# Taking the next pair's first gate step ahead of the down step in a streamed mixture-of-experts stage

## The reference

```python
D_EXPERT = D_MODEL // 8            # 256
N_EXPERTS = N_GROUPS * EXPERTS_PER_GROUP   # 32, two of them per token
...
h = h + hierarchical_moe(hn, w_router_group[i], w_router_expert[i],
                         w_expert_gate[i], w_expert_up[i], w_expert_down[i])
```

## Time and profile before

| | |
|---|---|
| time, median of 3 runs | 2208.81 us (2208.18 to 2210.3) |
| the profiled execution | 2207.76 us, of which 2206.0 us are the span |
| TensorE busy | 2156.0 us, 98% of the span |
| VectorE, ScalarE busy | 1314.9 us (60%), 900.7 us (41%) |
| mean granted TensorE clock | 0.996 |
| moved by DMA | 522.58 MB |

### The profile page before, as it was taken

One profiled execution on the slowest core, in us unless ns is written; L12 is line 12 of the kernel. 1 busy time (PEld: TensorE's weight loads), 2 busy tenths in 40 slices (PEclk: granted clock), 3 DMA queues, 4 the chain that ended last, 5 costly groups with the idle time before them and its releaser, 6 DMA issues.

```text
span 2206.0 us, 31962 instructions
## 1 busy us (share of the span) xinstructions
PE 2156.0 (98%) x12039; PEld 1707.9 (77%) x12039; DVE 1314.9 (60%) x1792; ACT 900.7 (41%) x1192; POOL 22.7 (1%) x42
## 2 busy tenths in 40 slices
PE   9999999999999899999999999999999999999998
PEld 8888888655555555888888888888888888888886
DVE  7797565432222225575667665678777777764444
ACT  5664454521111113554444454554444443433343
POOL 1000000000000000000000000000000000000000
PEclk9999999999999999999999999999999999999999
DMA  7566476899999999656655555556666666666664
GB/s 253 172 188 215 137 215 248 347 411 425 427 428 427 427 425 349 186 179 212 210 164 165 159 166 184 166 153 191 190 187 187 188 190 189 187 209 195 192 192 141
DMA packets 276768, 522.58 MB, mean 237 GB/s; under 512 B 21120, under 2 KB 193200, under 8 KB 261168
## 3 DMA queue, kind: packets, MB, share of 16 engines
q1 hardware_dynamic: 272128, 503.40, 66.8%
q0 software_dynamic: 4528, 17.63, 2.3%
HBM read 516.73 MB, written 7.36 MB: 238 GB/s over the span
## 4 chain that ended last, share of the span: by engine, by line
PE 84%; DMA 10%; DVE 4%; ACT 1%; issue 1%; SPq 0%; ACTq 0%; DVEq 0%
PE acc L784 30%; PE acc L805 24%; PE acc L808 12%; PE ps L1253 7%; DMA mw_late<-in_w_expert_gate 7%; DMA mw<-in_w_expert_up 3%; PE acc L1332 2%; DVE wlo L2135 1%; PE tp L893 1%; PE ps L961 1%; PE tp L1190 0%; PE tp L976 0%; PE ps L908 0%; PE tp L1200 0%; PE tp L990 0%
## 5 line engine op out<-in xcount | busy, mean ns | idle before, releaser
L2135 DVE TENSOR_TENSOR wlo<-raw,whi 128x1024 fp32r<-128x1024 f32 x568 | 671.0, 1221 | 207.1 <-ACT whi L1601 202.7
L805 PE MATMUL acc<-xhl,whi 128*128 128x512 f32 x2496 | 790.6, 398 | 1.6 <-DVE wlo L2135 0.7
L1601 ACT ACTIVATE whi<-raw 128x1024 fp32r<-128x1024 f32 x568 | 578.8, 1054 | 352.2 <-DMA raw<-in_w_down 131.9
L808 PEld LDWEIGHTS acc<-xhl,wlo 128*128 128x128 f32 x2496 | 468.9, 188 | 110.8
L808 PE MATMUL acc<-xhl,wlo 128*128 128x256 f32 x2496 | 490.8, 278 | 0.0
L805 PEld LDWEIGHTS acc<-xhl,whi 128*128 128x128 f32 x2496 | 381.4, 189 | 5.8 <-issue 3.0
L784 PE MATMUL acc<-whi,xhl 128*128 128x512 f32 x480 | 156.0, 395 | 0.0
L784 PE MATMUL acc<-whi,ah 128*128 128x512 f32 x336 | 130.7, 389 | 0.0
L784 PE MATMUL acc<-wlo,ah 128*128 128x512 f32 x336 | 130.7, 389 | 0.0
L784 PE MATMUL acc<-whi,al 128*128 128x512 f32 x336 | 130.7, 389 | 0.0
L1253 PE MATMUL ps<-mw,xg_turn 128*64 128x256 f32 x960 | 111.9, 386 | 12.9 <-DMA mw<-in_w_expert_up 12.9
(11 more groups left out here) (472 smaller groups left out, 2495.1 us busy)
## 6 DMA issues: line engine op xcount, KB each, us to landing
raw<-in_w_in SPq DMA_DIRECT2D x352, 256.0 KB, 3.0
raw<-in_w_up SPq DMA_DIRECT2D x352, 256.0 KB, 2.9
raw<-in_w_down SPq DMA_DIRECT2D x176, 256.0 KB, 3.2
mw<-in_w_expert_up SPq DMA_DIRECT2D x20, 2048.0 KB, 19.5
mw<-in_w_expert_down SPq DMA_DIRECT2D x20, 2048.0 KB, 18.7
raw<-in_w_out SPq DMA_DIRECT2D x128, 256.0 KB, 3.1
mw<-in_w_expert_up SPq DMA_DIRECT2D x24, 1024.0 KB, 11.3
mw<-in_w_expert_down SPq DMA_DIRECT2D x22, 1024.0 KB, 12.0
```

What stands on the lines that cost most here:

```text
L805: pe.matmul(out(ct).rearrange("p (m n) -> p m n", m=2), wh[:, ct * P:ct * P + P], ahl[:, :, k, :], start=first, stop=False, skip_group_che ...
L808: mm = pe.matmul(out(ct)[:, S:2 * S], wl[:, ct * P:ct * P + P], ahl[:, 0, k, :], start=False, stop=last, skip_group_check=True)
L1601: act.activation(whi[:, m % RING, :], raw[:, m % RING, :], ACT.Copy).then_inc(hi_ready, 1)
L2135: dve.tensor_tensor(wlo[:, m % RING, :], raw[:, m % RING, :], whi[:, m % RING, :], ALU.subtract).then_inc(lo_ready, 1)
```

## The change

TensorE does the first gate step of pair g+1 between `transpose(g)` with its moves and `down(g, 0)`, for every g+1 in `TURNED` (all pairs but 0 and 11). A step's place in TensorE's order is now its `RANK`, and waits on `w_used` go by it. SP loads in the order in which the steps are used (`LOAD_ORDER`): for the pairs of `WHOLE` that is up(g), gate(g+1), down(g), up(g+1). The loads by halves and the semaphore `w_half` are gone. In pair 0 the small matmuls of `weights` are spread between the matmuls of two gate/up steps, and `transpose(0)` goes into `gate_up(1, 0)`. A gate's first step waits for `silu_ready` in place of `hid_ready`, and the first up step waits for `hid_ready`.

```diff
-BY_HALVES = (5, 8, 12, 11, 13)
-HALF_USED = tuple(max(q for q in range(s) if PLACE[q] == PLACE[s]) for s in BY_HALVES)
+TURNED = [g for g in range(1, PAIRS) if g != OV_PAIR]
+USE_ORDER = []
+for _g in range(PAIRS):
+    USE_ORDER += [STEPS * _g + i for i in range(4) if i or _g not in TURNED]
+    USE_ORDER += [STEPS * (_g + 1)] if _g + 1 in TURNED else []
+    USE_ORDER += [STEPS * _g + 4, STEPS * _g + 5]
+RANK = {step: k + 1 for k, step in enumerate(USE_ORDER)}
+LOAD_ORDER = []
+for step in USE_ORDER:
+    if step not in LOAD_ORDER:
+        LOAD_ORDER += [step, step + 1] if step // STEPS in WHOLE and step % 2 == 0 else [step]
...
             def used_up(step):
 
-                if step // STEPS in WHOLE:
-                    return step // 2 * 2 + 2
-                return {6: 5, 4: 6, 5: 7}.get(step, step + 1)
+                return RANK[step // 2 * 2 + 1 if step // STEPS in WHOLE else step]
...
-                if step in BY_HALVES:
...
-            for step in (8, 9, 10, 12, 11, *range(13, N_STEPS - 2)):
+            for step in [q for q in LOAD_ORDER if FIRST_LATE < q < N_STEPS - 2]:
...
-            def weights():
+            def weights(g):
...
-            def gate_up(g, i):
+            def gate_up(g, i, beside=lambda k: None):
...
                 if g and c == 0:
+                    pe.wait_ge(silu_ready, g)
+                    pe.wait_ge(x_copied, 4 + 2 * g)
+                if g and c == 2:
                     pe.wait_ge(hid_ready, g)
-                    pe.wait_ge(x_copied, 4 + 2 * g)
...
-                if g != 1:
+                if g not in TURNED:
                     gate_up(g, 0)
...
                 gate_up(g, 1)
                 move(g, 0)
-                gate_up(g, 2)
-                move(g, 1)
-                gate_up(g, 3)
-                move(g, 2)
                 if g == 0:
-                    pe.wait_ge(slots_ready, 1)
-                    weights()
-                transpose(g)
-                move(g, 3)
-                if g == 0:
-                    gate_up(1, 0)
+                    gate_up(0, 2, weights)
+                    weights(7)
+                    gate_up(0, 3, lambda k: weights(8 + k))
+                    weights(15)
+                    gate_up(1, 0, lambda k: transpose(0) if k == 5 else None)
+                else:
+                    gate_up(g, 2)
+                    move(g, 1)
+                    gate_up(g, 3)
+                    move(g, 2)
+                    transpose(g)
+                    move(g, 3)
+                    if g + 1 in TURNED:
+                        gate_up(g + 1, 0)
...
-                act.wait_ge(w_used, STEPS * (g + 1) + (1 if g == 0 else 0))
+                act.wait_ge(w_used, RANK[STEPS * g + 5])
```

More of the change, by code:

```diff
@@ L73 @@
 WHOLE = range(5, PAIRS - 1)
-BY_HALVES = (5, 8, 12, 11, 13)
-HALF_USED = tuple(max(q for q in range(s) if PLACE[q] == PLACE[s]) for s in BY_HALVES)
-assert HALF_USED == (0, 1, 6, 4, 7)
+TURNED = [g for g in range(1, PAIRS) if g != OV_PAIR]
[9 more added lines that the diff above has]
+        LOAD_ORDER += [step, step + 1] if step // STEPS in WHOLE and step % 2 == 0 else [step]
 QK_ORDER = (0, 4, 1, 5, 2, 6, 3, 7)
@@ L356, in program @@
         fin_scaled = sem("fin_scaled")
-        y_half, w_half = sem("y_half"), sem("w_half")
+        y_half = sem("y_half")
         n_tp, n_hi, n_lo = sem("n_tp"), sem("n_hi"), sem("n_lo")
@@ L1213, in transpose @@
                 mm.then_inc(t_done, 1)
-            def weights():
[L1217 to L1222, removed]
+            weight_out = []
+            def weights(g):
+                if g == 0:
+                    pe.wait_ge(slots_ready, 1)
+                    weight_out.append(use())
+                o = weight_out[0]
+                for m in range(3 * TT):
+                    mm = pe.matmul(o[:, 2 * g:2 * g + 2], G[:, m % TT, pair_cols(g)], c3[:, m // TT, m % TT, 2 * g:2 * g + 2],
+                                   start=m == 0, stop=m == 3 * TT - 1, skip_group_check=True)
+                if g == PAIRS - 1:
+                    mm.then_inc(t_done, 1)
             def weights_of(g, i):
@@ L1255, in gate_up @@
                                        stop=c % 2 == 1 and k == 7, skip_group_check=True)
-                    if k == 3 and step in HALF_USED:
-                        mm.then_inc(w_half, 1)
+                    if k < 7:
+                        beside(k)
                 mm.then_inc(w_used, 1)
@@ L1333, in down @@
                                            skip_group_check=True)
-                        if (c, b) == (0, 1) and step in HALF_USED:
-                            mm.then_inc(w_half, 1)
                 mm.then_inc(w_used, 1)
```

## The result

The changed kernel took 2268.14 us in the median of 5 runs (2265.62 to 2270.35), the kernel before 2208.18 us beside it; the ratio is 1.0269, 95% interval 1.0258 to 1.0279. That is 60 us slower where 41 were forecast, and 4 us beyond the range. The profiled execution took 2267.69 us, 59.9 more than the one of before. The direction and, in the loop of the pairs of WHOLE, the mechanism are those of the forecast; its size is not, and the experiments are mostly about that.

A forecast was written before the change was run, and what follows sets the result against it. The stream of weights was taken to set the pace in pairs 5 to 14. Terms 34.9 + 4.5 + 1.7 + 0 = +41.1 us on 2208.81 gave 2249.9 us, range 2232 to 2264.

The forecast's parts named there:

- The loop of the WHOLE pairs: Pairs 5 to 14: late gate issue leaves the queue dry 5.0 us per loop; a pair takes 34.4 us, not 29.4.
- The count of the gaps: Gates of pairs 7 to 10, 13, 14 and step 90 of pair 15: 7 x 5.0 = 34.9 us.
- the stream stays full: Rival for the weight loads: SP finds slots free in time and nothing changes, 2208.4 us; chance 0.08.
- faster: Rival for the early loads: half loads had held the stream back, so -6.8 us, 2202.0 us; chance 0.06.
- The clock is held: Rival for TensorE: no lower clock behind the new waits, gaps of 3.3 us, +27.0, 2235.8 us; chance 0.15.
- the lower clock lasts: Rival for TensorE: lower clock through down and gate1 in each such pair, +108, 2317 us; chance 0.06.
- The price of a gap: Gates issued into a dry queue in WHOLE pairs: 2.45 us lost before the stream is full; 3.3 us dry.
- The clock: TensorE's down behind each 6 us idle runs at the lower clock: 1.7 us lost per loop, bounds 0 and 3.4.
- the small gap of pair 10: Pair 10's down load waits only for pair 9's down, 11.3 us against 9.8: a gap of 1.5 us.
- Round pair 11: Round the pair that isn't turned: gaps of 1.5 us at down(10) and 3.0 at pair 12's gates, sum 4.5.
- The opening: Early pairs: whole loads gain 1.8 us, new load order leaves 3.5 us dry; net +1.7, bounds -1.8 and +3.5.
- The tail: From pair 14's down to last_down: last_down again begins 18.1 us behind pair 15's second late gate load; cost nothing.

The follow-up runs named there:

- e1: The changed kernel with the gate step turned in pairs 1 to 4 alone: 2213.75 us, ratio 1.0026.
- e2: The changed kernel with both gate steps of the next pair ahead of its down steps: 2221.26 us, ratio 1.0061.
- e3: The changed kernel with WHOLE empty, so 1 MB loads and slots free by the step in every pair: 2216.3 us, ratio 1.0039.
- e9: The kernel before with half loads made whole, only pair 1's gate step turned, small matmuls in a block, step 12 loaded behind 10: ratio 1.0007.
- e8: The changed kernel with each 2 MB load of the pairs of WHOLE issued as two of 1 MB: 2272.42 us, ratio 1.0291.
- e13: The changed kernel with 24 small filler matmuls ahead of the wait for down in pairs 5 to 9 and 11 to 13: 2253.81 us, ratio 1.0213.
- e11: The kernel before with the 96 small matmuls spread between those of steps 2 and 3 of pair 0: 2211.73 us, ratio 1.0017.
- e7: The changed kernel with only pairs 1 to 4 turned and step 12 loaded behind step 10: 2212.86 us, ratio 1.0021.
- e6: The changed kernel with only pairs 1 to 4 turned and the small matmuls back in one block: 2212.05 us, ratio 1.0015.
- e10: The changed kernel with only pairs 1 to 4 turned, small matmuls in a block and step 12 loaded behind 10: ratio 1.0007.
- e14: The whole change with the small matmuls in a block and step 12 loaded behind step 10: 2264.05 us, ratio 1.0254.

## Why the prediction was right in its mechanism and wrong in its size

*The loop of the WHOLE pairs: right.* Slots that come free only behind gate1, SP holding up everything behind the gates, the queue dry behind up(g+1), TensorE idle 6 us (6.11 measured ahead of 647.82) and at the lower clock behind it: the trace shows each, and e1, e2 and e3 take the loss away in three ways, by not turning, by turning both, and by finer slots. The count of the gaps was right too: seven large ones, two smaller round pair 11. The rival "the stream stays full" fell on its own condition, and "faster" with e9. "The clock is held" fell with downs of 8.60 to 10.07 us, "the lower clock lasts" with gate1, which took 3.47 behind each of them. One thing no run separates: slots that come free late, and SP's order, in which down(g+1) stands behind the gates though its own slots are free 3.5 us earlier (620.96 against 624.44). Runs e1 to e3 take away both.

*The price of a gap: mis-sized.* The step "2.45 us are lost before the stream is full again", from one load of 1 MB, is the term of the sum that failed most. From the first issue to the last of four landings, seven runs of loads (the gates of pairs 7 to 10 and 12 to 14 and what follows them) took 22.4 to 23.4 us, in the mean 23.0, where 2.45 + 19.6 = 22.05 had been put. The first megabyte does land as the earlier trace rows says: in e8 the first load of 1 MB behind a dry queue took 4.9 to 5.2 us. But the first load of 2 MB in the changed kernel took 7.7 to 8.7 us, in the mean 8.0, for 4.9 us of data, so 3.1 of start. This is the one at 624.44:

```profile
mw_behind<-in_w_expert_gate SPq DMA_DIRECT2D x1, 2048.0 KB, 7.7
```

Most of the loss is there when the first 2 MB have landed; in the mean 0.4 us more come later in the run of four, in single runs between nothing and 1.0. e8 shows that the loss doesn't come from the size of the loads. The fit of the Trainium skill that I weighed (DMA: Bandwidth & Descriptors, Anatomy of one DMA: about 2.0 us beside the data, for loads issued from GpSimd) would have made the miss larger, and the trace disagrees: the loads read here behind a dry queue had 2.45 us or more beside their data. The advice of the Trainium skill to issue early and wait late (DMA: Bandwidth & Descriptors, Rules for kernel authors) named the direction, and the trace agrees: 427 GB/s fell to 365 and 362.

A likely reason, which no experiment tests, is unevenness of the 16 engines: a landing waits for the last of them, while those ahead take the next load's packets already. The stretches above show it at the end of up(7): most engines are through 8.4 us behind down(6)'s landing, where 9.8 were counted, and one or two work on for 2 us more. So down lands late against the mean of the engines, and measured from there the queue is through early.

*The clock: mis-sized.* I took 1.7 us for each loop with bounds of 0 and 3.4. The down steps ahead of the seven gaps took 9.43, 8.73, 9.70, 8.90, 10.07, 8.60 and 9.55 us, in the mean 9.28 against 7.02: 2.3 us. With pair 14's down, which I had taken at full clock and which took 8.78 (7.09 in e13), and the parts round pair 11, the clock is worth 12 to 14 us by e13. The forecast had 1.7 x 7 = 11.9 and 1.7 in the small gap of pair 10, 13.6. That term was nearly right in sum, though 0.6 us too small in each loop. What I hadn't seen is that the spells differ: the two longer waits of the earlier trace rows cost 1.7 each, and of these seven waits, 5.6 to 6.9 us long, the longest cost 1.6 and another 3.0.

*Round pair 11.* From the landing of down(9) to that of pair 12's gates and down(11) I had put 4.5 us. These twelve matrices take 67.6 us (719.30 to 786.87) against 59.4 before (689.44 to 748.82, there from the landing of pair 10's gates to that of pair 12's), 8.2 more. Both small gaps begin with a start that is dearer than 2.45 us (23.3 and 22.95 us for four loads), pair 9's down took 9.73 us, and pair 11's gates 8.83; how the 3.7 us over the forecast divide among these I haven't measured.

*The opening: wrong in its step.* I wrote "the small matmuls keep their count, 96 in 2.48 us, so spreading them moves no more than these 1.8 us". They don't keep their time. Between the gate matmuls a group of six took 0.23 us and the next four gate matmuls 0.58 where four take 0.43; with the two steps 12.7 us in place of 9.4. By e11 this alone costs 3.5 us. It also comes out that silu_ready, which I costed at nothing, is waited for 0.4 us there. The hole that I laid to the order of loads is there (357 GB/s), but the order alone doesn't mend it (e7), nor does the block alone (e6): it takes both (e10), since the spread small matmuls also delay the slot of step 10. In sum, e1 is 5.6 to 6 us above before, where the forecast had 1.7.

*The tail.* Forecast 0. last_down began at 916.12, 60.2 us later than before (855.97), while pair 14's down landed at 891.35; of the 24.8 us between, 1.8 are the lower clock in that down, behind an idle of 2.71 us, for which I had put nothing though the earlier trace rows shows 1.7 lost behind 2.14 and 2.42. The length of the idle alone doesn't say, though: in e13 the same down, with no filler in its pair, took 7.09 us behind an idle of 2.52.

The account by runs: 12 to 14 us clock (e13), 4 to 6 the opening (e14, e1), and the 40 or so that remain the dry queue at full clock: seven loops of 34.0 us in place of 29.4 are 32, and round pair 11 and in the first loop some 8. The forecast had 7 x 3.3 = 23 + 3 for the same. By the forecast's own terms, the 19 us that it missed are about 7 x 1.0 for the start, 7 x 0.6 for the clock in the loops, 4 for the opening, 3.7 round pair 11 and 1.8 in the tail; these come to 21, 2 more than there are to explain.

## What to carry to other kernels

Before a step of the order is turned, ask of each slot which step sets it free, and then what the issuing queue holds behind the load that waits for it: here one step of 3.5 us, moved past a wait, emptied a queue that had 12 us of stock. When a stream runs dry, count the start of a run of loads from the first issue to the last landing (3.4 us beside the data here), not from one small load (2.45), and count the clock behind the new idle too. Small matmuls put between large ones aren't free, even where their own count and time are small.

## What the runs showed of the hardware that I had not expected

- 6 matmuls of 2 columns and the 4 gate matmuls behind them take 0.81 us interleaved, where the same work apart is 0.43 + 0.16 = 0.59 (96 in 2.48 us).
- After an idle of 5.6 to 6.9 us, at the lower clock, the same down step took between 8.6 and 10.1 us in one execution: the loss isn't a constant. After an idle of 2.71 us it took 8.78 in the changed kernel, after one of 2.52 it took 7.09 in e13.
- Of four 2 MB loads issued into an idle queue, the last landed 22.4 to 23.4 us after the first issue, for 19.6 us of data at 427 GB/s. The first landed after 7.7 to 8.7 us, for 4.9 us of data. Splitting the loads into halves left the whole as it was (22.6 to 23.7).
- 48 calls of a 128x128 float32 matmul are 96 instructions of 0.114 us, 10.92 us in all.
